# Conditioning of a hybrid decoder layer: eight output tiles per accumulation, one K tile per piece, and six turns instead of 24

## The chip, the cores and the metric

The kernel runs on one core of a Trainium2 chip. A core has five engines that each run their own list of instructions in order and meet only at semaphores: TensorE (PE, with its weight loads shown as PEld), VectorE (DVE), ScalarE (ACT), GpSimd (POOL) and SyncE (SP), which here only issues transfers. Sixteen DMA engines move data between the memory (HBM) and the on-chip memory (SBUF). Matrix products land in PSUM, in banks that hold 512 floats for each of 128 partitions. The metric is the device time in microseconds (us), median of several runs.

## The reference

One inference step of one decoder layer on 1024 prompt rows and 8 sample rows, width 1024, all in float32. Every sequence has a conditioning vector `c` (1 prompt and 8 samples, so 9 of them), from which shift, scale and gate of both halves of the layer come:

```python
mod = jax.nn.silu(c) @ w_ada + b_ada                  # (9, 1024) @ (1024, 6144)
sh1, sc1, gt1, sh2, sc2, gt2 = jnp.split(mod[:, None, :], 6, axis=-1)
h = rmsnorm(x, norm1_g) * (1.0 + sc1) + sh1
proj = h @ w_in                                       # then RG-LRU, mLSTM and pooling groups
...
mix = jnp.concatenate([y_a, y_b, y_c], axis=-1) @ w_out
x = x + gt1 * mix
h2 = rmsnorm(x, norm2_g) * (1.0 + sc2) + sh2
x = x + gt2 * (jnp.square(jax.nn.relu(h2 @ w_ff1)) @ w_ff2)
y = rmsnorm(x, final_g)
```

`w_ada` is 25 MB, read once. The change touches only how `mod` is computed.

## The kernel before, in words

Activations lie feature-major: 8 feature tiles (KT) of 128 partitions by 1032 tokens, in three chunks of 344 tokens. The big products run in float32r as three products (high by high, low by high, high by low) of tiles called H_hi, H_lo, W_hi, W_lo (L2407 to L2409), into banks called D. `WV` are the weights of the value heads (L2434 to L2436).

The conditioning gives 48 output tiles (NADA) of 128 features by 9 vectors. The weight tile of one output tile is 128 partitions (the K rows of one K tile) by 8 K tiles by 128 features, in HBM as 128 rows of 4096 bytes, 512 KB in all. The kernel before works in 24 pairs of output tiles, and each pair in two halves of four K tiles. A **piece** is one such half: 2 tiles by 4 K tiles by 128 features for each partition, 512 KB, which `load_raw` (L556) reads as rows of 2048 bytes into one of four slots of a ring called RAWW. The same ring also carries the weight tiles of the big products (L561).

In `ada` (L2378) TensorE uses its four groups of 32 columns: group j holds the vectors of K tile j as its weights (CTX, 32 columns wide, 9 of use) and streams the 256 features of the pair. The four groups write partitions 0, 32, 64 and 96 of one bank, and the second half adds onto the first. So the bank holds four partial sums, 9 rows each, by 256 features. ScalarE copies this to ADS (L1297). Two small products, the **turn** (`ada_turn`, L2392), multiply ADS with SEL, a 128 by 9 matrix made once from the identity (L1710), which both turns the result to features by vectors and adds the four partial sums. VectorE adds the bias and writes MOD (`modulation`, L1717); for the scales it then makes (1 + scale) times the norm's weight (L1719).

The order of all work in the first third is written out by hand in the text MIX_ORDER and read by every engine: `ADA:i:h` is a piece (on ScalarE the copy to ADS after the last piece of a group), `ADT` the turn, `ADM` the modulation, `SQ` and `NS` the sum of squares and the norm of a chunk (L1763, L2398, L1257, L1742), `N:c:k` the normalised tile k of chunk c (L1728, L1251, L1252, L1087), `DK:u:c:a:b` K tiles a to b of the dense product of unit u and chunk c, `D` all eight, `W` and `WV` the split of weights in high and low parts, `V` the value heads, `R:n` the load of ring entry n by ScalarE's queue. The rest are steps of the mixers. The first 20 pieces are loaded by SP, each as soon as the piece four before it has been used (`raw_used`), with the tokens (X0T, L802), the first weight tiles (WR, L822) and WV_raw (L817) at fixed places between them (SP_AFTER); the other 28 by ScalarE's queue.

The first 16 output tiles (shift 1 and scale 1) are needed before the first normalised tile; the program starts with their 16 pieces, pairs in the order 0, 4, 1, 5, 2, 6, 3, 7. The other 32 tiles are spread over the dense products that follow, up to about 370 us. The banks X0 to X4 serve all small products; the function `bank_uses` hands them out: pairs in X3 or X4, turns in X1 at the start and in X3 later.

Of the kernel before, what the change touches and what calls it, by code (L numbers as in the profile page):

```python
# [17 lines left out]
ALU = mybir.AluOpType  # L18
# [5 lines left out]
P = 128  # L24
D = 1024
# [26 lines left out]
AH = KT // 2  # L52
NPAIR = NADA // 2
ADA_START = (0, 4, 1, 5, 2, 6, 3, 7)
ADA_FIRST = 2 * len(ADA_START)
# [10 lines left out]
N_SP_RAW = 2 * len(ADA_START) + RAW  # L66
# [21 lines left out]
def unit_of(kind, t):  # L88
# [4 lines left out]
ADA:0:0 ADA:0:1 SQ:0:0 ADA:4:0 ADA:4:1 SQ:0:1 SQ:1:0 ADT:0 ADM:0 ADA:1:0 SQ:1:1 ADA:1:1 ADT:4 ADM:4 NS:0  # L93
ADA:5:0 ADA:5:1 N:0:0 ADT:1 ADM:1 N:0:1 ADA:2:0 ADA:2:1 ADT:5 ADM:5 ADA:6:0 ADA:6:1 ADT:2 ADM:2 N:0:2 ADA:3:0 W:0
    ADA:3:1 ADT:6 N:0:3 W:1 ADM:6 ADA:7:0 ADA:7:1 ADT:3 N:0:4 N:0:5 ADM:3 ADT:7 ADM:7 N:0:6 N:0:7 NS:1
DK:0:0:0:6
WV:0 DK:1:0:0:6
DK:0:0:6:8
WV:1 WV:2 DK:1:0:6:8
ADA:8:0  # L100
# [31 lines left out]
D:4:1 LRUM:0
D:4:2 R:34 W:6
D:5:0 ADT:12 ADM:12 ADA:13:0 ADA:13:1 R:33 LRUC:1
D:5:1
D:5:2 ADT:13 R:35 ADM:13 ADA:14:0 LRUG:1 ADA:14:1
D:6:0 R:37 W:7 ADT:14 LRUA:1 R:36 R:38 ADM:14
D:6:1 LRUM:1
D:6:2 R:40 ADA:15:0
D:7:0  # L140
D:7:1 W:8 ADA:15:1 LRUC:2 R:39
D:7:2 ADT:15 LRUG:2 LRUA:2
D:8:0 R:41 ADM:15 ADA:16:0 W:9
# [24 lines left out]
D:16:0 R:65 HM:7 Y:6 U:7 YD:6 CN:7 ADM:23
# [5 lines left out]
def plan_mix():  # L174

    raws = [("ADA", i, h) for i in ADA_START for h in range(2)]
    pairs = [i for i in range(NPAIR) if i not in ADA_START]
    early, pairs = pairs[:2], pairs[2:]
    raws += [("ADA", i, h) for i in early for h in range(2)]
    for u in range(3, N_MIX):  # L180
        raws += [("W", u)] + [("ADA", pairs[u - 3], h) for h in range(2)]
    assert len(pairs) == N_MIX - 3
# [15 lines left out]
def bank_uses(plan):  # L198
# [8 lines left out]
    for s in plan:  # L207
# [5 lines left out]
        elif k == "ADA" and s[2] == 0:  # L213
            add(("ADA", s[1]), "X3" if s[1] in ADA_START[::2] else "X4")
# [75 lines left out]
def build(nc, I, O):  # L290
# [13 lines left out]
    ADA_ORDER = [k[1] for k in raw_seq if k[0] == "ADA" and k[2] == 0]  # L304
# [10 lines left out]
    with ExitStack() as ctx:  # L315
# [88 lines left out]
        ADS, SEL = at("ADS", [P, 2 * P], rSB), new("SEL", [P, DEC + 1])  # L404
# [87 lines left out]
        ada_half = sem("ada_half")  # L492
        win_lower = [sem(f"windows{j}_lower") for j in range(POOL_T)]
        win_upper, win_joined = sem("windows0_upper"), [sem(f"windows{j}_joined") for j in range(POOL_T)]
        ld_idn, sel_ready = sem("ld_idn"), sem("sel_ready")
# [56 lines left out]
        def load_raw(e, n):  # L552
            key = raw_seq[n]
            if key[0] == "ADA":
                w = AH * P
                e.dma_start(RAWW[:, n % RAW, :].rearrange("p (e n) -> p e n", e=2),  # L556
                            I["WADA"][2 * key[1]:2 * key[1] + 2, :, key[2] * w:(key[2] + 1) * w].rearrange("e p n -> p e n")
                            ).then_inc(raw_in[n % RAW], 16)
            else:
                u = key[1]  # L560
                e.dma_start(RAWW[:, n % RAW, :], I["W"][in_unit(u)]).then_inc(raw_in[n % RAW], 16)  # L561

        def raw_used(e, n):
# [649 lines left out]
        def _(act):  # L1213
# [55 lines left out]
            for s in plan:  # L1269
# [22 lines left out]
                elif k == "ADA" and s[2]:  # L1292
                    i, key = ADA_ORDER.index(s[1]), ("ADA", s[1])
                    if i:
                        wait_full(act, ("ADT", ADA_ORDER[i - 1]))
# [381 lines left out]
        def _(dve):  # L1677
# [32 lines left out]
            V.tensor_reduce(SEL[:], IDN[:].rearrange("p (j i) -> p i j", j=P // 32)[:, 0:DEC + 1, :], AX_X, ALU.add).then_inc(sel_ready, 1)  # L1710

            def modulation(key):

                j, (bk, n) = 2 * key[1], use[key]
                wait_full(dve, key)
                ps = XB[bk][:, 0:32].rearrange("p (e b) -> p e b", e=2)[:, :, 0:DEC + 1]
                put_free(V.tensor_tensor(MOD[:, j:j + 2, :], ps, wide(col("b_ada", j, 2), DEC + 1), ALU.add), key)  # L1717
                if j // KT in (1, 4):
                    link(V.scalar_tensor_tensor(out=MOD[:, j:j + 2, :], in0=MOD[:, j:j + 2, :], scalar=1.0,  # L1719
                                                in1=wide(col("g1" if j < 2 * KT else "g2", j % KT, 2), DEC + 1), op0=ALU.add, op1=ALU.mult))  # L1720
# [638 lines left out]
        def _(pe):  # L2359
# [12 lines left out]
            def ada(i, half):  # L2372

                raw = raw_wait(pe, ("ADA", i, half))
                ps = take(("ADA", i)) if half == 0 else bank(("ADA", i))
                for j in range(AH):
                    k = (AH * half + j) * (DEC + 1)
                    one = T.matmul(ps[32 * j:32 * j + 32, 0:2 * P], CTX[:, k:k + 32],  # L2378
                                   RAWW[:, raw, :].rearrange("p (e k n) -> p e k n", e=2, k=AH)[:, :, j, :],
                                   start=(half == 0), stop=(half == 1), tile_position=(0, 32 * j))  # L2380
                if half:
# [504 lines left out]
```

## Time and profile before

| | |
|---|---|
| median of 3 runs | 1174.8 us (1170.45, 1174.8, 1176.62) |
| profiled execution | 1175.78 us, span 1174.0 us |
| PE busy | 1124.6 us (96%) |
| DVE, ACT, POOL busy | 792.8, 473.4, 346.9 us |
| mean granted clock of TensorE | 0.982 of full |
| HBM read, written | 96.81 MB, 12.18 MB |

The span runs from the first to the last instruction. TensorE is busy 96% of it, so what it does not do in the first 50 us (where transfers are the limit), and what it does beside the big products after that, is what the conditioning can cost. A busy time counts overlapped instructions once; a `matmul` instruction in float32 appears as two records, so one turn (two products) is four records and one piece (four products) eight.

### The profile page before, as it was taken

The numbers are of one execution on the slowest core, as the hardware profiler recorded it, in microseconds if no ns is written. First come the engines' busy times: TensorE is split into PE (matmuls) and PEld (weight loads), VectorE is DVE, ScalarE is ACT, GpSimd is POOL, SyncE is SP. The second block draws the span as 40 slices with busy tenths as digits, with TensorE's granted clock in tenths as the row PEclk, the third lists the DMA queues.
The fourth block names the chain that finished last, engine by engine and source line by source line (L and its number), as shares of the span: only waits on it lengthen the run. The fifth ranks groups of instructions, "written<-read, shape, count | busy, mean of one in ns | idle before, by whom it ended". The sixth has DMA issues, their size and how long they took to land.

```text
span 1174.0 us, 19681 instructions
## 1 busy us (share of the span) xinstructions
PE 1124.6 (96%) x7237; PEld 1077.3 (92%) x7237; DVE 792.8 (68%) x1319; ACT 473.4 (40%) x780; POOL 346.9 (30%) x275
## 2 busy tenths in 40 slices
PE   4799999999989999999999999999999999999997
PEld 1598888888979999899999999999999999999996
DVE  4561455478775434678578878778778788788546
ACT  5551355655456344642233332332432433433431
POOL 0442011201434357764032022132131231231352
PEclk9699999998989999999999999999999999999998
DMA  8912523566523722111111111202102202111104
GB/s 302 326 57 88 142 90 126 177 180 218 176 87 113 269 90 73 54 55 37 37 36 55 54 37 55 71 18 71 56 16 75 68 18 72 53 50 58 37 1 145
DMA packets 67846, 109.85 MB, mean 94 GB/s; under 512 B 6435, under 2 KB 42567, under 8 KB 67399
## 3 DMA queue, kind: packets, MB, share of 16 engines
q1 hardware_dynamic: 57574, 84.88, 22.0%
q10 hardware_dynamic: 10208, 24.12, 6.6%
q8 instruction: 41, 0.67, 0.2%
q14 instruction: 23, 0.18, 0.0%
HBM read 96.81 MB, written 12.18 MB: 93 GB/s over the span
## 4 chain that ended last, share of the span: by engine, by line
PE 82%; DVE 9%; ACT 3%; DMA 2%; issue 1%; POOL 1%; SPq 1%; ACTq 0%; POOLq 0%; DVEq 0%
PE D L2407 7%; PE D L2409 7%; PE D L2408 7%; PE D L2591 6%; PE D L2593 5%; PE D L2592 5%; PE X L2593 5%; PE X L2591 5%; PE X L2592 5%; PE X L2663 5%; PE X L2664 5%; PE X L2665 5%; PE D L2663 2%; PE D L2665 2%; PE D L2664 2%; DMA RAWW<-in_WADA 2%
## 5 line engine op out<-in xcount | busy, mean ns | idle before, releaser
L2407 PE MATMUL D<-H_hi,W_hi 128*128 128x344 f32 x472 | 158.6, 336 | 3.7 <-POOL H_lo L1087 3.1
L2409 PE MATMUL D<-H_hi,W_lo 128*128 128x344 f32 x472 | 152.4, 323 | 0.0
L2408 PE MATMUL D<-H_lo,W_hi 128*128 128x344 f32 x472 | 152.4, 323 | 0.0
L1087 POOL TENSOR_TENSOR Y_lo<-FU,Y_hi 128x344 fp32r<-128x344 f32 (+3 forms) x84 | 100.1, 1194 | 154.2 <-ACT Y_hi L1521 88.5
L1082 POOL TENSOR_TENSOR W_lo<-RAWW,W_hi 128x1024 fp32r<-128x1024 f32 x25 | 61.6, 2465 | 182.5 <-ACT W_hi L1234 182.2
L1087 POOL TENSOR_TENSOR Y_lo<-EY,Y_hi 128x344 fp32r<-128x344 f32 (+1 forms) x24 | 38.3, 1598 | 216.3 <-ACT Y_hi L1521 144.5
L2407 PEld LDWEIGHTS D<-H_hi,W_hi 128*128 128x128 f32 x472 | 90.5, 192 | 11.8 <-issue 7.6
L2408 PEld LDWEIGHTS D<-H_lo,W_hi 128*128 128x128 f32 x472 | 90.3, 191 | 0.9 <-issue 0.5
L2409 PEld LDWEIGHTS D<-H_hi,W_lo 128*128 128x128 f32 x472 | 90.2, 191 | 0.0
L2215 DVE SCALAR_TENSOR_TENSOR X<-X,MOD 128x344 f32<-128x344 f32 (+1 forms) x138 | 75.7, 566 | 9.2 <-PE X L2665 9.0
L2663 PE MATMUL X<-Y_hi,W_hi 128*128 128x344 f32 x252 | 80.7, 320 | 0.0
L2664 PE MATMUL X<-Y_lo,W_hi 128*128 128x344 f32 x252 | 80.6, 320 | 0.0
L2665 PE MATMUL X<-Y_hi,W_lo 128*128 128x344 f32 x252 | 80.5, 319 | 0.0
L2017 DVE SCALAR_TENSOR_TENSOR X<-D,MOD,X 128x344 f32<-128x344 f32 (+1 forms) x72 | 41.3, 573 | 45.4 <-PE D L2593 24.7
L2407 PE MATMUL D<-Y_hi,W_hi 128*128 128x344 f32 x192 | 62.0, 323 | 1.5 <-POOL W_lo L1082 1.5
L1099 POOL TENSOR_TENSOR SS<-SS,SQ 128x344 f32<-128x344 f32 x45 | 43.3, 963 | 65.9 <-ACT SQ L1430 40.5
L1087 POOL TENSOR_TENSOR Y_lo<-KEPT,Y_hi 128x344 fp32r<-128x344 f32 x24 | 26.4, 1098 | 120.7 <-ACT Y_hi L1521 120.7
L2408 PE MATMUL D<-Y_lo,W_hi 128*128 128x344 f32 x192 | 61.3, 319 | 0.0
L2409 PE MATMUL D<-Y_hi,W_lo 128*128 128x344 f32 x192 | 61.3, 319 | 0.0
L1556 ACT ACTIVATE W_hi<-RAWW 128x1024 fp32r<-128x1024 f32 x30 | 31.8, 1059 | 64.3 <-PE X L2665 55.6
L2378 PE MATMUL X<-RAWW,CTX 128*32 128x256 f32 x384 | 35.7, 461 | 19.5 <-DMA RAWW<-in_WADA 19.4
L1087 POOL TENSOR_TENSOR H_lo<-FU,H_hi 128x344 fp32r<-128x344 f32 (+2 forms) x33 | 29.9, 914 | 66.2 <-ACT FU L1252 50.7
(416 smaller groups left out, 3455.1 us busy)
## 6 DMA issues: line engine op xcount, KB each, us to landing
RAWW<-in_W SPq DMA_DIRECT2D x76, 512.0 KB, 3.6
RAWW<-in_WADA ACTq DMA_DIRECT2D x28, 512.0 KB, 4.1
RAWW<-in_WADA SPq DMA_DIRECT2D x20, 512.0 KB, 8.0
RAWW<-in_W ACTq DMA_DIRECT2D x18, 512.0 KB, 3.7
X0T<-in_x SPq DMA_DIRECT2D x3, 1376.0 KB, 12.8
out_y<-OUTN SPq DMA_DIRECT2D x24, 172.0 KB
X<-in_x SPq DMA_DIRECT2D x8, 344.0 KB, 5.3
NM<-nm_d SPq DMA_DIRECT2D x8, 256.0 KB, 5.3
```

Source lines behind the costliest of these rows:

```text
L1082: nc.gpsimd.tensor_tensor(lo_v, RAWW[:, raw, :] if src is None else src[:], hi_v.bitcast(F32), ALU.subtract).then_inc(w_lo_ready, 1)
L1087: nc.gpsimd.tensor_tensor(lo_v, fu_v, hi_v.bitcast(F32), ALU.subtract).then_inc(lo_ready, 1)
L2215: V.scalar_tensor_tensor(out=X[:, m, c * CH:c * CH + w], in0=ps[:, 0:w], scalar=MOD[:, 5 * KT + m, 0:1], in1=X[:, m, c * CH:c * CH + w], o ...
L2407: T.matmul(out, w_h, hi[:, kt, a:b], start=(kt == 0), stop=False)
L2408: T.matmul(out, w_h, lo[:, kt, a:b], start=False, stop=False)
L2409: one = T.matmul(out, w_l, hi[:, kt, a:b], start=False, stop=(kt == KT - 1))
L2591: T.matmul(out, w_h, hi(kt), start=(kt == 0 and not onto), stop=False, skip_group_check=onto)
L2592: T.matmul(out, w_h, lo(kt), start=False, stop=False, skip_group_check=onto)
L2593: one = T.matmul(out, w_l, hi(kt), start=False, stop=(kt == n - 1), skip_group_check=onto)
L2663: T.matmul(bank[:, 0:CH], w_hi[:, a:a + P], h, start=(start and k == 0), stop=False, skip_group_check=onto)
L2664: T.matmul(bank[:, 0:CH], w_hi[:, a:a + P], l, start=False, stop=False, skip_group_check=onto)
L2665: one = T.matmul(bank[:, 0:CH], w_lo[:, a:a + P], h, start=False, stop=(stop and k == 1), skip_group_check=onto)
```

## The change

A group now is eight output tiles, and a piece is one K tile of all eight: group j of TensorE's columns streams tiles 2j and 2j+1, 256 features, all with the same weights, the vectors of this K tile. Eight pieces add up in the bank (K is summed wholly in PSUM), so the four column groups hold four finished pairs of output tiles and no partial sums. There are 6 groups of 8 pieces (48 pieces, as before), 6 copies to ADS, 6 turns and 6 modulations. The turn now picks columns 0 to 8, 32 to 40, 64 to 72 and 96 to 104 of the identity, 36 columns, and SEL is gone. The modulation writes 72 columns at once. The first two groups hold the even and the odd ones of the first 16 output tiles.

A piece has the same 512 KB, but its rows in HBM are now 512 bytes (one K tile of 128 features of one output tile), 1024 of them instead of 256 of 2048 bytes. The output tiles of one piece lie 512 KB apart, in the first two groups 1 MB.

```diff
-AH = KT // 2
-NPAIR = NADA // 2
-ADA_START = (0, 4, 1, 5, 2, 6, 3, 7)
+K_PIECE = 1
+GROUPS = 4 // K_PIECE
+ADA_T = 2 * GROUPS
+N_PIECE = KT // K_PIECE
+N_ADA = NADA // ADA_T
+N_START = 2 * KT // ADA_T
...
-ADA:0:0 ADA:0:1 SQ:0:0 ADA:4:0 ADA:4:1 SQ:0:1 SQ:1:0 ADT:0 ADM:0 ADA:1:0 SQ:1:1 ADA:1:1 ADT:4 ADM:4 NS:0
...
+ADA:0:0 ADA:0:1 SQ:0:0 ADA:0:2 ADA:0:3 SQ:0:1 SQ:1:0 ADA:0:4 ADA:0:5 SQ:1:1 NS:0 ADA:0:6 ADA:0:7 ADT:0 ADM:0
...
-DK:0:0:0:6
-WV:0 DK:1:0:0:6
-DK:0:0:6:8
-WV:1 WV:2 DK:1:0:6:8
+DK:0:0:0:1 DK:0:0:2:3 DK:0:0:4:5 DK:0:0:6:7 DK:0:0:1:2 DK:0:0:3:4
+WV:0 DK:1:0:0:1 DK:1:0:2:3 DK:1:0:4:5 DK:1:0:6:7 DK:1:0:1:2 DK:1:0:3:4
+DK:0:0:5:6 DK:0:0:7:8
+WV:1 WV:2 DK:1:0:5:6 DK:1:0:7:8
...
         elif k == "ADT":
-            add(s, "X1" if s[1] in ADA_START else "X4" if s[1] == NPAIR - 1 else "X3")
+            add(s, "X1" if s[1] < N_START else "X4" if s[1] == N_ADA - 1 else "X3")
...
-                add(("TS", w), ("X3", "X4")[w])
+                add(("TS", w), ("X3", "X2")[w])
...
+    def ada_tiles(q):
+
+        return slice(q, 2 * KT, N_START) if q < N_START else slice(ADA_T * q, ADA_T * (q + 1))
...
-                w = AH * P
-                e.dma_start(RAWW[:, n % RAW, :].rearrange("p (e n) -> p e n", e=2),
-                            I["WADA"][2 * key[1]:2 * key[1] + 2, :, key[2] * w:(key[2] + 1) * w].rearrange("e p n -> p e n")
+                w = K_PIECE * P
+                e.dma_start(RAWW[:, n % RAW, :].rearrange("p (t n) -> p t n", t=ADA_T),
+                            I["WADA"][ada_tiles(key[1]), :, key[2] * w:(key[2] + 1) * w].rearrange("t p n -> p t n")
...
-            V.tensor_reduce(SEL[:], IDN[:].rearrange("p (j i) -> p i j", j=P // 32)[:, 0:DEC + 1, :], AX_X, ALU.add).then_inc(sel_ready, 1)
...
+            def ada(q, piece):
+
+                raw = raw_wait(pe, ("ADA", q, piece))
+                ps = take(("ADA", q)) if piece == 0 else bank(("ADA", q))
+                w = RAWW[:, raw, :].rearrange("p (t h n) -> p t h n", t=ADA_T, h=K_PIECE)
+                for j in range(4):
+                    g, h = j // K_PIECE, j % K_PIECE
+                    k = (piece * K_PIECE + h) * (DEC + 1)
+                    one = T.matmul(ps[32 * j:32 * j + 32, 0:2 * P], CTX[:, k:k + 32], w[:, 2 * g:2 * g + 2, h, :],
+                                   start=(piece == 0), stop=(piece == N_PIECE - 1), tile_position=(0, 32 * j))
...
+                pick = IDN[:].rearrange("p (g b) -> p g b", g=GROUPS)[:, :, 0:DEC + 1]
                 for e in range(2):
-                    one = T.matmul(ps[:, 16 * e:16 * e + DEC + 1], ADS[:, e * P:(e + 1) * P], SEL[:], start=True, stop=True)
+                    out = ps[:, 64 * e:64 * e + GROUPS * (DEC + 1)].rearrange("p (g b) -> p g b", g=GROUPS)
+                    one = T.matmul(out, ADS[:, e * P:(e + 1) * P], pick, start=True, stop=True)
```

**The start, on TensorE.** The program of before, from its first piece (X<-RAWW,CTX, eight rows for two pieces) to the first dense product (D<-H_hi,W_hi):

```order
L2378 MATMUL X<-RAWW,CTX 32x256 x16
L2392 MATMUL X<-SEL,ADS 128x9 x2
L2378 MATMUL X<-RAWW,CTX 32x256 x8
L2392 MATMUL X<-SEL,ADS 128x9 x2
L2398 MATMUL X<-SS,ONE 128x344
L2378 MATMUL X<-RAWW,CTX 32x256 x8
...
L2378 MATMUL X<-RAWW,CTX 32x256 x8
L2392 MATMUL X<-SEL,ADS 128x9 x4
L2398 MATMUL X<-SS,ONE 128x344
L2407 MATMUL D<-H_hi,W_hi 128x344
```

And the same stretch now, where the two rows of the identity (X<-IDN,ADS) are the turns of the first and the second group:

```order
L2386 MATMUL X<-RAWW,CTX 32x256 x24
L2407 MATMUL X<-SS,ONE 128x344
L2386 MATMUL X<-RAWW,CTX 32x256 x8
L2401 MATMUL X<-IDN,ADS 128x36 x2
L2386 MATMUL X<-RAWW,CTX 32x256 x32
L2401 MATMUL X<-IDN,ADS 128x36 x2
L2407 MATMUL X<-SS,ONE 128x344
L2416 MATMUL D<-H_hi,W_hi 128x344
```

Eight turns have become two, the sum of squares of the first chunk stands after six pieces, and the second turn and the sum of squares of the second chunk stand between the last piece and the first dense product.

**The start, on VectorE.** Before, from the sums of squares (SS) to the end of the first chunk's normalised tiles (FU), each modulation (MOD) between them:

```order
L1763 TENSOR_TENSOR SS<-SS,SQ 128x344 x12
L1717 TENSOR_TENSOR MOD<-X,COLS 128x18
L1763 TENSOR_TENSOR SS<-SS,SQ 128x344 x4
L1717 TENSOR_TENSOR MOD<-X,COLS 128x18
L1719 SCALAR_TENSOR_TENSOR MOD<-MOD,COLS 128x18
L1742 RECIPROCAL X<-SS 128x344
L1728 SCALAR_TENSOR_TENSOR FU<-X0T,MOD,X 128x344
...
L1728 SCALAR_TENSOR_TENSOR FU<-X0T,MOD,X 128x344
L1732 TENSOR_SCALAR FU<-FU,MOD 128x344
L1742 RECIPROCAL X<-SS 128x344
```

And now:

```order
L1769 TENSOR_TENSOR SS<-SS,SQ 128x344 x16
L1748 RECIPROCAL X<-SS 128x344
L1720 TENSOR_TENSOR MOD<-X,COLS 128x8x9
L1726 SCALAR_TENSOR_TENSOR MOD<-MOD,COLS 128x4x9
L1734 SCALAR_TENSOR_TENSOR FU<-X0T,MOD,X 128x344 x4
L1738 TENSOR_SCALAR FU<-FU,MOD 128x344
L1720 TENSOR_TENSOR MOD<-X,COLS 128x8x9
L1726 SCALAR_TENSOR_TENSOR MOD<-MOD,COLS 128x4x9
L1734 SCALAR_TENSOR_TENSOR FU<-X0T,MOD,X 128x344 x4
L1738 TENSOR_SCALAR FU<-FU,MOD 128x344
L1748 RECIPROCAL X<-SS 128x344
```

The four even tiles of the first chunk follow the first modulation, the four odd ones the second.

**Later, on TensorE.** One of the 12 turns that go after the start, before: it stands between a product of the mLSTM and its next one (VB_105 is a buffer of values, KW the weighted keys).

```order
L2392 MATMUL X<-SEL,ADS 128x9 x2
L2528 MATMUL X<-VB_105,KW 96x97 x4
L2378 MATMUL X<-RAWW,CTX 32x256 x4
L2498 MATMUL X<-IDN,K_1_102 128x96 x4
L2502 MATMUL X<-Q_1_104,K_1_102 128x128 x4
```

And now:

```order
L2537 MATMUL X<-VB_105,KW 96x97 x4
L2386 MATMUL X<-RAWW,CTX 32x256 x4
L2507 MATMUL X<-IDN,K_1_102 128x96 x4
L2511 MATMUL X<-Q_1_104,K_1_102 128x128 x4
```

The turn is gone, and each piece stands where one stood before.

## Rows read from the trace of the kernel before

**Rows 1.** Busy time by stretch: us, each engine's, clock, DMA share, GB/s.
```profile
4.00:22.00 18.00, 7.45 (x52) 2.16 (x52) 7.98 (x23) 9.40 (x20) 0.00 (x0) 1.00 1.05 379
...
24.00:26.00 2.00, 2.00 (x17) 0.60 (x16) 0.75 (x4) 1.83 (x2) 0.00 (x0) 1.00 0.73 238
26.00:28.00 2.00, 1.92 (x25) 0.94 (x20) 2.00 (x1) 0.38 (x1) 0.00 (x0) 1.00 0.42 143
28.00:30.00 2.00, 0.75 (x8) 0.69 (x12) 1.73 (x6) 1.11 (x3) 0.00 (x0) 0.90 0.63 235
30.00:36.00 6.00, 1.23 (x12) 0.23 (x12) 0.10 (x1) 1.16 (x3) 1.83 (x2) 0.50 0.94 320
...
60.00:235.00 175.00, 170.72 (x1111) 152.14 (x1109) 81.94 (x146) 79.67 (x137) 36.72 (x25) 1.00 0.36 114
235.00:345.00 110.00, 100.14 (x731) 93.42 (x730) 86.25 (x175) 53.30 (x75) 25.95 (x19) 0.96 0.52 163
```

**Rows 2.** Chain of waits, 0 to 62 us: start, us, what.
```profile
28.80 10.01 DMA RAWW<-in_WADA
...
41.13 2.00 DVE MOD L1719
...
45.45 1.35 PE X L2398 x2
46.79 0.29 PE D L2407
```

**Rows 3.** Timeline around the last piece of the start: start, us, engine, line, what.
```profile
36.69 1.02 PE L2392 MATMUL X<-SEL,ADS 128*128 128x9 f32 x4
...
40.81 1.94 PE L2378 MATMUL X<-RAWW,CTX 128*32 128x256 f32 x16
...
41.44 0.43 PEld L2378 LDWEIGHTS X<-RAWW,CTX 128*32 128x32 f32 x8 [0.42 <-DMA RAWW<-in_WADA]
```

**Rows 4.** Busy time by stretch, while only rows of 512 bytes were read.
```profile
258.00:258.25 0.25, 0.25 (x4) 0.25 (x3) 0.21 (x2) 0.00 (x0) 0.00 (x0) 1.00 1.05 317
258.25:258.50 0.25, 0.25 (x3) 0.25 (x2) 0.22 (x2) 0.00 (x0) 0.00 (x0) 1.00 1.06 312
258.50:258.75 0.25, 0.25 (x4) 0.25 (x3) 0.22 (x2) 0.00 (x0) 0.00 (x0) 1.00 1.14 346
```

**Rows 5.** DMA view of 257.0 to 259.5 us, two such loads from first to last.
```profile
DMA packets 899, 0.55 MB, mean 219 GB/s; under 512 B 32, under 2 KB 899, under 8 KB 899
```

**Rows 6.** Line L1297, all records: duration ns min/median/max, first and last start.
```profile
L1297 ACT ACTIVATE ADS<-X x24: 358/384/385, 12.8 to 365.4; 128x256 f32<-128x256 f32 x24
```

**Rows 7.** Timeline of TensorE around one turn at 140 us.
```profile
140.04 0.32 PE L2409 MATMUL D<-H_hi,W_lo 128*128 128x344 f32 x1
140.19 0.51 PE L2392 MATMUL X<-SEL,ADS 128*128 128x9 f32 x4
140.55 0.40 PE L2407 MATMUL D<-H_hi,W_hi 128*128 128x344 f32 x1
140.79 0.32 PE L2408 MATMUL D<-H_lo,W_hi 128*128 128x344 f32 x1
```

**Rows 8.** Waits of TensorE, 100 to 385 us: us in total, times, longest.
```profile
PE X L2549 <- DVE NUM L1903: 3.7, 1, 3.7
...
PE X L2536 <- DVE MOD L1717: 1.5, 1, 1.5
...
PE X L2392 <- DVEq L1941: 0.9, 1, 0.9
...
PE X L2392 <- DVE QK L1875: 0.4, 1, 0.4
PE X L2458 <- DVE MOD L1717: 0.3, 1, 0.3
```

**Rows 9.** Lines L962 and L966, all transfers of each, from issue to landing.
```profile
DMA to landing us min/median/max: 3.3/3.5/4.7
DMA to landing us min/median/max: 3.4/3.6/4.4
```

More of the change, by code:

```diff
@@ L132 @@
+D:1:2 ADA:2:4 G1 ADA:2:5
+D:2:0 R:24
+D:2:1 R:26 G2
+D:2:2 R:28 W:4 G3 ADA:2:6 R:27 R:29
+D:3:0 ADA:2:7 G4
+D:3:1 R:31 ADT:2 LRUC:0
+D:3:2 ADM:2 W:5 ADA:3:0
+D:4:0 R:30 ADA:3:1 LRUG:0 R:32 LRUA:0
 D:4:1 LRUM:0
 D:4:2 R:34 W:6
-D:5:0 ADT:12 ADM:12 ADA:13:0 ADA:13:1 R:33 LRUC:1
+D:5:0 ADA:3:2 ADA:3:3 R:33 LRUC:1
 D:5:1
-D:5:2 ADT:13 R:35 ADM:13 ADA:14:0 LRUG:1 ADA:14:1
-D:6:0 R:37 W:7 ADT:14 LRUA:1 R:36 R:38 ADM:14
+D:5:2 R:35 ADA:3:4 LRUG:1 ADA:3:5
+D:6:0 R:37 W:7 LRUA:1 R:36 R:38
 D:6:1 LRUM:1
-D:6:2 R:40 ADA:15:0
+D:6:2 R:40 ADA:3:6
@@ L174, in plan_mix @@
 def plan_mix():
[L176 to L179, printed above, removed]
+    pieces = [("ADA", q, k) for q in range(N_ADA) for k in range(N_PIECE)]
+    raws, pieces = pieces[:N_SP_RAW], pieces[N_SP_RAW:]
     for u in range(3, N_MIX):
-        raws += [("W", u)] + [("ADA", pairs[u - 3], h) for h in range(2)]
-    assert len(pairs) == N_MIX - 3
+        raws += [("W", u)] + pieces[2 * (u - 3):2 * (u - 2)]
+    assert len(pieces) == 2 * (N_MIX - 3)
     out = []
@@ L213, in bank_uses @@
         elif k == "ADA" and s[2] == 0:
-            add(("ADA", s[1]), "X3" if s[1] in ADA_START[::2] else "X4")
+            add(("ADA", s[1]), "X3" if s[1] < N_START and s[1] % 2 == 0 else "X4")
         elif k == "ADT":
-            add(s, "X1" if s[1] in ADA_START else "X4" if s[1] == NPAIR - 1 else "X3")
+            add(s, "X1" if s[1] < N_START else "X4" if s[1] == N_ADA - 1 else "X3")
         elif k in ("G1", "G2", "G3", "G4", "Y", "YS"):
@@ L403, in build @@
         CTS = at("CTS", [P, CW], rH)
-        ADS, SEL = at("ADS", [P, 2 * P], rSB), new("SEL", [P, DEC + 1])
+        ADS = at("ADS", [P, 2 * P], rSB)
         COLS, IDN, ONE = new("COLS", [P, NCOLS]), new("IDN", [P, P]), new("ONE", [P, P])
@@ L1291, in _ @@
                     load_raw(act, s[1])
[L1292 to L1295, printed above, removed]
+                elif k == "ADA" and s[2] == N_PIECE - 1:
+                    key = ("ADA", s[1])
+                    if s[1]:
+                        wait_full(act, ("ADT", s[1] - 1))
                     wait_full(act, key)
@@ L2370, in done @@
                 ins.then_inc(x_full[use[key][0]], 1)
[L2372 to L2381, printed above, removed]
-                    done(one, ("ADA", i))
+            def ada(q, piece):
[7 more added lines that the diff above has]
+                                   start=(piece == 0), stop=(piece == N_PIECE - 1), tile_position=(0, 32 * j))
+                if piece == N_PIECE - 1:
+                    done(one, ("ADA", q))
                 else:
-                    one.then_inc(ada_half, 1)
+                    one.then_inc(ada_piece, 1)
             def ada_turn(key):
```

100 lines of the change are left out of this document (47 added, 53 removed).

## The prediction

> **What bounds the kernel now.** I read the busy time by stretch first, then the chain of waits, then TensorE's waits and its timeline around the turns. There are three regimes. In the first 46 us TensorE waits for transfers: from 4 to 22 us the 16 DMA engines are full, 379 GB/s at a share of 1.05 [rows 1], and a wait of 10.01 us for a piece lies on the chain [rows 2]. From 60 to 235 us TensorE itself is the bound, busy 170.72 of 175.00 us; from 235 to 345 us it is busy 100.14 of 110.00 us [rows 1] and shares the bound with VectorE, for which it waits up to 3.7 us at a time [rows 8]. After 385 us nothing of the conditioning is left and nothing moves. So the change has two sides: the start, where only bytes, rows of transfers and the tail behind the last piece count, and the middle, where each instruction taken off TensorE counts.
>
> **The middle, what goes.** 24 copies to ADS [rows 6] go with 24 turns. Eight are at the start, 16 later; now 2 and 4. So 12 turns leave the middle. What one costs is read where nothing waits: from the start of the product before it, 140.04, to the second product behind it, 140.79, is 0.75 us [rows 7]. Two products without a turn would take two steps of 0.15 to 0.16 (the first row and the turn start 0.15 apart), 0.32 us. A turn costs 0.43 us, and 12 cost 5.2 us. With them go waits that only a turn has, or that its bank makes for others: 0.9 and 0.4 us before a turn, 1.5 us where a transpose of HM waits for the modulation to free X3, 0.3 us where the gate transposes do [rows 8]; 3.1 us together. Upper bound: 8.3 us.
>
> Not all of it reaches the end. Two of the 12 turns (at about 241 and 321 us in the timeline) stand where TensorE comes too early for VectorE anyway, and the wait of 3.7 us for NUM [rows 8] shows that a TensorE ahead of time finds VectorE late. I take off two turns, 0.9 us, and keep 7.4 us. Lower bound: 7 of the 12 turns lie before 235 us, where TensorE is the bound, 3.0 us. The four turns that stay stream 36 columns instead of 9; I cost this at nothing, since the weights (128 columns, twice per product) are loaded as before and cover it, and at most 0.1 us each if they don't. VectorE loses 18 modulations and ScalarE 18 copies of 0.384 us [rows 6]; beside TensorE, they only help the waits counted.
>
> **The middle, what comes.** 32 pieces, less the four that SP loads, now are 1024 rows of 512 bytes each. Before, from 258.00 to 258.75 us only rows of 512 bytes were moved, back to back: 317, 312 and 346 GB/s, mean 325, at a share of 1.05 to 1.14 [rows 4]. A piece has 524,288 bytes: 1.38 us at 379 GB/s, 1.61 us at 325, so 0.23 us more. 32 of them hold the engines 7.4 us longer. The share is 0.36 before 235 us and 0.52 in the mLSTM stretch [rows 1], where keys, queries and the values of a chunk come by the same engines. TensorE waited for no piece there. If every added microsecond met a waiting load, it would be 7.4 times 0.52, 3.8 us; if none, 0. I take +1.0, nearer to none, for no piece was late.
>
> **The start.** The first dense product needs all 16 pieces, as before, for the turn of the second group stands ahead of it. The pieces are 8.39 MB beside 3.9 MB of tokens and weights. 16 times 0.23 is 3.7 us more of transfer. Against it stands a hole: from 24 to 30 us the engines moved 238, 143 and 235 GB/s instead of 379 [rows 1], a shortfall of 141, 236 and 144 GB/s over 2 us each, or 2.7 us of full transfer. It came from the ring: SP loads a piece when the one four before it is used, and TensorE sat behind turns, a modulation and the sum of squares. In the new order six pieces stand before the sum, and no turn stands between pieces 1 and 8, so I expect the hole to be filled. Last piece: +1.0 us, between 2.1 - 2.7 = -0.6 (at 346 GB/s) and +3.7 (nothing filled).
>
> Then the tail. The last piece was there at 41.4 us [rows 3], and dense products flow alone from 46.79 [rows 2]: 5.4 us, with two turns, a modulation that took 2.00 us [rows 2] and the sum of squares in between. Now: the piece 1.0 us (two took 1.94 [rows 3]), the copy 0.38 [rows 6], one turn 1.02 [rows 3], the sum 1.35 [rows 2], some 0.3 for the semaphores between: 4.1 us, so -1.3. These are prices at the low clock level: the granted clock is 0.50 from 30 us [rows 1], that is 1.2 GHz, after TensorE had little to do, and I expect the same again. What the odd tiles add: four instead of two normalised tiles are still open when the dense products begin. The first dense products use the even tiles, 12 products at 0.29 us [rows 2], 3.5 us; an odd tile comes after the modulation (2.0 us if it meets GpSimd again) and the steps of one tile on three engines. That is a near thing, and the norm of the second chunk and WV_lo come behind it. Bounds 0 and +2; I take +0.8, the lower half, since the even tiles stand first. The start: +1.0 - 1.3 + 0.8 = +0.5 us.
>
> A rule of the Trainium skill bears on this term, DMA: Bandwidth & Descriptors, "Why small descriptors are slow (HBM only)": a packet costs about three cycles beside one for each 32 bytes. By it 2048 bytes take 67 cycles and four times 512 take 76, 13% more; the rows of this trace say 17% (379 against 325). As an estimate from that page, the last piece would come 1 us earlier than by the rows.
>
> **Sum.** -7.4 + 1.0 + 0.5 = -5.9 us against the profiled execution, 1175.8 us: 1169.9. The median of the runs shown lies 1.0 us lower, 1174.8; so 1168.9, say 1169.
>
> **Rivals.**
> *A slower start, and a slower kernel.* The rows of 512 bytes of one partition lie 512 KB or 1 MB apart, and the rate may fall under what the back-to-back stretch showed. The price: over the whole of two such loads the mean was 219 GB/s, with their beginning and end in it [rows 5]. At that rate a piece takes 2.39 us, 1.01 more; 16 of them 16.2 us, less the hole 2.7 and the tail 1.3, plus 0.8: start +13.0, in all -7.4 + 1.0 + 13.0 = +6.6, 1181.4 on the scale of the median. The kernel gets slower from the point where a piece takes 0.60 us more, at 265 GB/s. Against it: line L966 loads rows 1 MB apart of 1024 bytes, and they land in 3.6 us, 0.1 more than whole rows of 4096 [rows 9].
> The Trainium skill speaks for it, same page, "Latency and other measured facts", on a row pitch of large powers of two: 207 GB/s at a pitch of 512 KiB, 164 at 2 MiB, against 214. As an estimate from this page, a piece of the start would take up to 1.3 times as long as its rows say, some 2.1 us; rows 9 don't show it at a pitch of 1 MB.
> *The turns come off TensorE, and VectorE gives nothing.* Only the 7 turns before 235 us count: -3.0 + 0.5 + 1.0 = -1.5, 1173.3. For it: the wait on NUM in that stretch, VectorE busy 86.25 of 110.00 us. Against it: VectorE is fed by TensorE, and loses work as well.
> *Everything comes through.* -8.3, the start at its good end -0.6 - 1.3 = -1.9, no late loads: -10.2, 1164.6. For it: 96% busy TensorE overall. Against it: it needs three good ends at once.
> That the change doesn't do what it says, fewer turns, I exclude: TensorE's program has the 6.
>
> **How the numbers follow.** Forecast 0.43, own range 1166 to 1172. Slower start 0.13. VectorE gives nothing 0.28. Everything 0.16. A measurement of this kernel can tell about 0.5%, 5.9 us, from no change: below 1168.9 is faster, above 1180.7 slower. The forecast lies on that line; I give 0.25 of its 0.43 to faster and 0.18 to same, since its unpriced remainders (turns at the low clock) go down. Faster: 0.25 + 0.16 = 0.41. Slower: 0.11 of the slower start's 0.13. Same: 0.18 + 0.28 + 0.02 = 0.48. The range 1163.5 to 1179.5 reaches past "everything" and towards the slower start, without its end.
>
> **What would show it.** The rate from 4 to 22 us: 325 to 340 GB/s, and no hole from 24 to 30. The last piece of the start at 42 to 43 us, TensorE's first dense product alone at 47 to 48. Six copies to ADS. At 235 us the same work 2.5 to 3.5 us earlier than before; at 385 us about 6 us earlier. A piece in the first 50 us at 2 us or more makes the slower start right; a lead at 235 us of 3 us that is gone by 385 makes VectorE the one that took it. Waits of TensorE for pieces after 60 us, or longer ones for keys and values, would say that +1.0 was too little.

## The result, and the profile after

The changed kernel takes 1180.77 us (median of 13 runs, 1175.48 to 1183.6), the kernel before 1174.39 beside it: ratio 1.0044, interval [1.0029, 1.006]. It is 5 to 6 us slower where 6 us faster was forecast, and lies outside the range. The interval lies wholly above 1: a small loss, but a clear one. The profiled execution took 1181.2 us, its span is 1179.3; before they were 1175.8 and 1174.0.

The step was made as described. ScalarE copies ADS six times:
```profile
L1300 ACT ACTIVATE ADS<-X x6: 374/383/386, 28.2 to 370.9; 128x256 f32<-128x256 f32 x6
```

The busy time by stretch (columns as in [rows 1]) shows the new rate of the transfers, and where the clock fell:
```profile
4.00:22.00 18.00, 4.77 (x39) 1.04 (x40) 7.36 (x21) 8.31 (x16) 0.00 (x0) 1.00 1.12 324
...
24.00:26.00 2.00, 2.00 (x14) 0.66 (x10) 0.90 (x2) 1.64 (x3) 0.00 (x0) 1.00 1.20 289
26.00:28.00 2.00, 1.93 (x16) 0.25 (x12) 1.40 (x1) 0.50 (x1) 0.00 (x0) 1.00 1.20 290
...
60.00:235.00 175.00, 167.66 (x1071) 149.34 (x1069) 80.52 (x138) 79.99 (x134) 38.98 (x26) 1.00 0.37 112
235.00:345.00 110.00, 104.48 (x726) 97.46 (x727) 83.88 (x161) 49.34 (x66) 24.67 (x18) 0.91 0.58 169
345.00:385.00 40.00, 36.13 (x228) 31.90 (x227) 27.39 (x55) 23.99 (x39) 17.57 (x16) 0.91 0.38 107
```
The hole from 24 to 28 us is gone (before 238 and 143 GB/s, [rows 1]), but it is filled at 290 GB/s, with the engines at a share of 1.20. A piece of 524,288 bytes takes 1.81 us at that rate, not the 1.61 of [rows 4]; before, in a stretch with nothing but pieces of 2048-byte rows, the rate was 388 GB/s:
```profile
20.00:22.00 2.00, 1.61 (x16) 0.20 (x8) 1.82 (x5) 1.58 (x5) 0.00 (x0) 1.00 1.06 388
```

The chain of waits at the end of the start (start us, us, what):
```profile
28.99 8.45 DMA RAWW<-in_WADA
...
38.62 6.19 DMA RAWW<-in_WADA
...
44.85 1.13 PE X L2386 x8
...
46.06 0.39 ACT ADS L1300
...
46.50 1.07 PE X L2401 x4
47.57 1.30 PE X L2407 x2
48.87 0.29 PE D L2416
```
The last piece lands at 44.81 us instead of 41.4. Behind it stand 4.06 us to the dense products (forecast 4.1), which flow from 48.87 us instead of 46.79. (The profile of before is a late one here: two other profiles of the old order with 2048-byte rows have this product 1.2 and 1.5 us earlier, so the start may have lost up to 3.6 us.)

How far the same product of TensorE lies from its place before, read from the two timelines (us, minus is earlier):
```
place before    57    100   126-150  155-205   209-218  226   241   262   288   312   325   385 to the end
after          +2.3  +1.7   +0.5    -0.7..+0.1  +0.9   -0.3  +4.8  +3.4  +3.1  +1.6  +5.6   +5.6
```
So up to 205 us the fewer turns paid back the 2.3 us that the start had lost. Then 5.9 us were lost between 226 and 325 us. Nothing moves behind 385 us, as forecast.

TensorE's waits, 100 to 385 us (us in total, times, longest), against [rows 8]:
```profile
PE X L2529 <- DVE EX L1901: 3.9, 2, 2.2
PE X L2558 <- DVE NUM L1909: 3.7, 1, 3.7
PE X L2507 <- DMA VB<-v_d: 2.9, 1, 2.9
...
PE X L2551 <- DVE KW L1898: 1.3, 1, 1.3
```
For each chunk of the mLSTM, EX are the weighted scores, KW the weighted keys and NUM the numerators of its output, all three made by VectorE, and VB are its values, loaded from HBM. Two rows of before belong beside these:
```profile
PE X L2520 <- DVE EX L1895: 2.9, 3, 1.7
PE X L2498 <- DMA VB<-v_d: 0.9, 1, 0.9
```
The waits that belonged to turns and modulations are gone. What is left is VB, 2.9 us, at 235 us (0.9 before, at 244); EX, 2.2 us, at 272 (1.7 before, at 268); KW, 1.3 us, at 318, which is new; EX, 1.7 us, at 341; and NUM, 3.7 us, at 350, as before. From 200 to 360 us all waits together are 12.9 us, where they were 10.9. At four of them, VB, EX at 272, KW and NUM, the granted clock is at its lower level, 0.50 (1.2 GHz), the first three here:
```profile
232.00:237.00 5.00, 2.09 (x27) 1.44 (x20) 0.75 (x3) 1.59 (x2) 0.00 (x0) 0.99 0.77 188
237.00:243.00 6.00, 5.99 (x30) 5.18 (x23) 4.01 (x10) 0.63 (x1) 0.00 (x0) 0.50 1.08 328
...
271.00:277.00 6.00, 5.29 (x24) 5.30 (x25) 4.03 (x10) 2.26 (x3) 1.65 (x1) 0.50 0.55 186
277.00:318.00 41.00, 39.91 (x304) 36.50 (x302) 36.93 (x69) 18.38 (x27) 9.55 (x7) 0.99 0.78 228
318.00:325.00 7.00, 6.83 (x31) 6.84 (x32) 4.89 (x11) 2.29 (x2) 4.66 (x4) 0.56 0.08 24
```
Each of these low stretches lasts some 7 us, and there products take twice the time: 3.5 us more where TensorE has work all the while. The profile of before has two of the four, at EX (268.5 to 275.5 us) and at NUM (343.5 to 350.5). Those at VB and KW are new. Summed as (1 - granted clock) over stretches of 1 us from 200 to 360 us, the profile after has lost at most 13.7 us, that of before 6.8. So the two new low stretches, 6.9 us, weigh more than the 2.0 us of longer waits. One execution is a sample only: the kernel's own runs lie 8 us apart.

### The profile page after: what moved, and what is told of

Read it like the earlier page. It is cut to its first block, busy times and chain, and to the rows that moved or that the text cites. A ratio compares the mean times of both kernels' runs of the same rounds, so it can differ in the third digit from the quotient of the medians.

```text
span 1179.3 us, 19438 instructions
## 1 busy us (share of the span) xinstructions
PE 1122.1 (95%) x7165; PEld 1072.1 (91%) x7165; DVE 789.4 (67%) x1295; ACT 467.5 (40%) x762; POOL 347.8 (29%) x275
## 4 chain that ended last, share of the span: by engine, by line
PE 79%; DVE 9%; DMA 4%; ACT 4%; POOL 1%; issue 1%; SPq 1%; ACTq 0%; POOLq 0%; DVEq 0%
PE D L2416 6%; PE D L2418 6%; PE D L2417 6%; PE D L2600 6%; PE D L2602 5%; PE D L2601 5%; PE X L2602 5%; PE X L2600 5%; PE X L2601 5%; PE X L2672 5%; PE X L2673 5%; PE X L2674 5%; DMA RAWW<-in_WADA 3%; PE D L2672 2%; PE D L2674 2%; PE D L2673 2%
## 5 line engine op out<-in xcount | busy, mean ns | idle before, releaser
L1102 POOL TENSOR_TENSOR SS<-SS,SQ 128x344 f32<-128x344 f32 x45 | 43.3, 963 | 65.9 <-ACT SQ L1433 40.5
L2386 PEld LDWEIGHTS X<-RAWW,CTX 128*32 128x32 f32 x384 | 8.5, 119 | 45.5 <-DMA RAWW<-in_WADA 28.7
```

## Experiments

**The size of the rows, in either order.** Only the layout of the weights on the host and the source of the transfer change:
```diff
-                            I["WADA"][ada_tiles(key[1]), :, key[2] * w:(key[2] + 1) * w].rearrange("t p n -> p t n")
+                            I["WADA"][N_PIECE * key[1] + key[2]].rearrange("h p n -> p h n")
```
with h = 2 (2048 bytes), h = 1 (4096), or h = 8 (512 bytes, but 64 KB apart). In the kernel before, the same is done the other way: the four K tiles and two output tiles of a piece are read as eight rows of 512 bytes, 512 KB apart, or as one of 4096.

> The changed kernel, whose pieces lie on the host so that a row has 2048 bytes (two per partition) as before the change; bytes, order, products and turns are those of the changed kernel. Theory rows (the 512-byte rows cost the time): a piece takes 1.38 instead of 1.81 us, the last piece of the start lands at 38 to 40 us instead of 44.8, the dense products flow alone at 43 to 45, the values' piece waits less at 235 us, and the time is 1165 to 1169, 12 to 16 us less than the changed kernel. Rival order (where the pieces and turns stand in the middle costs it, not their rows): only the start moves, 4 to 5 us, 1176. Rival turns (they never gave anything): not under 1174.

> The changed kernel with rows of 512 bytes still, but the eight rows of a partition lie 64 KB apart and those of neighbouring partitions one behind the other, where in the changed kernel they lie 1 MB (start) or 512 KB (later) and 4 KB apart. Theory number of rows: a piece of the start takes 1.8 us as in the changed kernel, 290 GB/s from 22 to 30 us, and the time is 1179 to 1182. Rival pitch: the rate is that of the 512-byte stretch of the kernel before, 325 GB/s or more, a piece 1.61 us, the last piece of the start 3 us earlier, the time 1175 to 1178.

> The kernel before, with all its 24 turns and its own order, but its pieces come in rows of 512 bytes (eight per partition, 512 KB apart) as in the changed kernel. Theory rows: a piece takes 1.8 us instead of 1.38, 16 of them 6.9 us more, of which the hole from 24 to 30 us takes some 2.7: start +4 to +5, and the middle +1 to +6; the time is 1179 to 1185. Rival order: only the start's part, 1177 to 1179, and no wait of 2 us or more for a transfer of the values near 235 us.

> The kernel before with its pieces laid out so that each partition reads one row of 4096 bytes (before: two of 2048). Theory rows: if 512 to 2048 bytes gives 290 to 379 GB/s, the next doubling gives at most 3 per cent, a piece 0 to 0.05 us less, the time 1172 to 1175. Rival: rows of 2048 still cost at the start, the last piece lands 1 us or more earlier, 1172 or less.

Measured, as ratio to the kernel before:
```
rows of      order before             order after
512 bytes    1.0036 [1.0023, 1.0050]  1.0044 [1.0029, 1.0060]   (64 KB apart: 1.0057 [1.0035, 1.0080])
2048         1                        0.9970 [0.9953, 0.9988]
4096         0.9983 [0.9968, 0.9998]  0.9968 [0.9949, 0.9986]
```
With 2048-byte rows the change makes the kernel faster, 1170.56 us, 10 us less than with 512 (9 by the ratios). The expectation's 1165 to 1169 was too good by 2. Read along a line of the table, with the same rows in both orders, the new order is worth -1 us with 512-byte rows (within the intervals), 3.5 us with 2048 and 2 us with 4096 (its intervals overlap). So with short rows nearly the whole loss against the kernel before is theirs: the old order loses 4 us by them as well. Stretches of before_rows512, after_rows512_near and after_rows2048, one row each:
```profile
22.00:24.00 2.00, 1.28 (x12) 0.20 (x8) 1.79 (x6) 1.70 (x4) 0.00 (x0) 1.00 1.20 291
```
```profile
22.00:24.00 2.00, 1.27 (x16) 0.20 (x8) 1.69 (x5) 1.59 (x5) 0.00 (x0) 1.00 1.20 290
```
```profile
4.00:22.00 18.00, 6.81 (x49) 1.64 (x50) 8.91 (x25) 9.74 (x20) 0.00 (x0) 1.00 1.04 380
```
290 GB/s belongs to the row of 512 bytes in both orders, and it is the same whether the rows of a partition lie 1 MB or 64 KB apart. The rival of the pitch falls. The figures that the prediction cites from the Trainium skill (DMA: Bandwidth & Descriptors, "Latency and other measured facts") are for a large pitch from one partition's row to the next; here those rows lie 4 KB and 512 bytes apart, so no run here tests them, and they didn't bear on this rival. The rule of the Trainium skill on small packets (DMA: Bandwidth & Descriptors, "Why small descriptors are slow (HBM only)") had the direction. The prediction's reading of it, 13% more, was less than half of what was measured: pieces land 1.80 us apart with 512-byte rows and 1.36 with 2048, 33% more. (The 380 GB/s above has the tokens in it; over the same 18 us the changed kernel moved 324.)

**Where the long rows count.**
```diff
+                if n < N_SP_RAW:        # after_long_later: n >= N_SP_RAW
+                    e.dma_start(RAWW[:, n % RAW, :], I["WADAP"][N_PIECE * key[1] + key[2], 0]
+                                ).then_inc(raw_in[n % RAW], 16)
+                else:
```

> The changed kernel, where the 20 pieces that SP loads (16 of the start, 4 of the next group) come as one row of 4096 bytes per partition and the 28 later ones as 512-byte rows as in the changed kernel. Theory both ends (the start pays 6 of the 10 us between short and long rows, the mLSTM stretch the rest): start 4.1 us before that of the kernel before, 6.5 at 205 us, then 2 to 4 us given up from 235 to 345 us; 1172 to 1176. Rival start alone: all of the 10 us lie in the start, the time is that of long rows everywhere, 1170 to 1171.

> The other half: the 20 pieces that SP loads come in 512-byte rows as in the changed kernel, the 28 later ones as one row of 4096 bytes per partition. Theory both ends: start 2.2 us late as in the changed kernel, level with the kernel before at 205 us, and nothing or 2 us lost from 235 to 345 us; 1175 to 1178. Rival start alone: as the changed kernel, 1180 to 1181.

> The changed kernel with all pieces as one row of 4096 bytes per partition. Theory: 390 instead of 380 GB/s at the start, dense products alone at 41.5 to 43 us, otherwise as with rows of 2048; 1168 to 1171. Rival: rows of 2048 have all there is, 1170.5 again. Beside after_long_start and after_long_later it says whether their two gains add up.

Measured: long rows at the start 1171.52 (0.9984 [0.9972, 0.9997]), only later 1178.57 (1.0030 [1.0012, 1.0047]), everywhere 1171.79 (0.9968 [0.9949, 0.9986]). By the ratios the start is worth 7 us, the later pieces 1.6 to 1.9 (the medians give 9.3 and 2.2, and 0 with a long start). The profiles agree. In the six of the changed order with 4096-byte rows at the start (and no products added there) the first dense product starts at 40.5 to 43.5 us, 41.9 in the mean (by the timeline, which has it 0.7 us ahead of the chain above); in the five with 512-byte rows at 48.0 to 48.5. That is 6.3 us. The start decides, as the rival had it, and the later rows cost 0 to 2 us: the +1.0 of the forecast was about right.

**The wait for the values.** SP loads VB of chunk 0 before it waits for the last queries:
```diff
                     if c == 0:
+                        for i in range(2):
+                            sp.wait_ge(v_stored[i], 16 * NLC // 2)
+                        sp.dma_start(VB[0][:].rearrange("p h v -> p (h v)"), v_d[0]).then_inc(ld_kqv[0], 16)
```

> The changed kernel with 512-byte rows; SP loads the values of the first chunk (VB) before it waits for the last queries to be stored, some 5 us earlier, and K, Q and NM as before. Theory wait: TensorE's wait of 2.9 us for VB at 235 us goes, K and Q then bound it; 1.5 to 2.5 us of the loss in the mLSTM stretch come back, 1178 to 1179.5. Rival: K or Q land no earlier and the wait goes over to them, or VectorE takes it, 1180 to 1181.

> The changed kernel with rows of 4096 bytes and the values of the first chunk loaded before the wait for the last queries. Theory wait: TensorE's waits for VB at 223 to 238 us go, and with them a drop of the clock; 1 to 2.5 us less than with rows of 4096 alone, 1169 to 1171. Rival: K and Q bound it at the same place, 1171 to 1172.

Measured: 1178.22 with 512-byte rows (1.0041 [1.0028, 1.0055]), 1170.87 with 4096 (0.9962 [0.9944, 0.9981]), both within the intervals of the kernels without the edit. The medians lie 2.6 and 0.9 us lower, in the theory's ranges, but each stands against its own runs of the kernel before, and the ratios differ by 0.0003 and 0.0006 only: the times don't tell. The wait for VB is gone from both profiles. In its place TensorE waits 1.1 us for EX at the next step, and in the second one 2.2 us for EX at 258 us. By the traces the rival is right: take one wait away, and the next one on VectorE's side ends last.

**Products in place of waits.** If the loss is the low clock behind the waits, TensorE must not stand still there. 50 products with zeros are added, which change no value:
```diff
+            FILL = {("S", 0): 6, ("S", 1): 6, ("AB", 0): 6, ("AB", 2): 4, ("YS",): 10, ("AB", 6): 8, ("POOL", 0, 0): 10}
+            def fill(s):
+                for _ in range(FILL.get(s, 0)):
+                    T.matmul(XB["X4"][:, 0:P], IDN[:], ZERO[:, 0:1].to_broadcast([P, P]), start=False, stop=False)
...
+                    fill(s)
                     pe.wait_ge(x_free[bk], n + 1)
```

> The changed kernel (512-byte rows) with 50 products of the identity with zeros (128 columns each, some 0.16 us) that TensorE makes where it waited in the changed order's mLSTM stretch: 6 ahead of K of chunks 0 and 1, 6 and 4 ahead of EX of chunks 0 and 2, 10 ahead of the HS transposes, 8 ahead of EX of chunk 6, 10 ahead of the first pool product. They add zeros to the open sum in X4. Theory clock (TensorE comes early, waits for VectorE or for VB, and behind each such wait its clock is granted at 0.50 for 3.4 to 7 us, which costs more than the wait): the waits are filled, the granted clock between 230 and 345 us stays 1.00 but for one drop at most, and 3 to 5 us come back, 1176 to 1178. Rival: the products come on top, 8 us of them where 10 us of waits were; the time is 1180 to 1184.

> The same 50 products in the changed kernel with rows of 4096 bytes. Theory clock: 2 to 4 us come back, 1168 to 1170, and the scatter between executions (1163.7 to 1174.2 without) gets smaller, for it would come from how long the clock stays low. Rival: they come on top, 1173 to 1176.

> Rows of 4096 bytes, values early, and the 50 products together. Theory clock: the best of these, 1166 to 1169. Rival: no better than rows of 4096 alone, 1171 to 1173.

Measured: with rows of 4096 bytes 1166.31 (1164.53 to 1167.77; 0.9928 [0.9904, 0.9951]), with the values early as well 1165.38 (0.9916 [0.9891, 0.9941]). The products take 5.5 us off the kernel with rows of 4096 bytes (4.7 by the ratios), and the spread of its runs shrinks from 10.6 us (12 runs) to 3.2 (6 runs). The same place in the timelines, after_rows4096 first:
```profile
301.73 0.64 PE L2386 MATMUL X<-RAWW,CTX 128*32 128x256 f32 x8
304.39 0.32 PE L2551 MATMUL X<-IDN,HS 8*128 8x8 f32 x3 [2.02 <-DVE KW L1898]
```
```profile
301.77 2.50 PE L2410 MATMUL X<-ZERO,IDN 128*128 128x128 f32 x20
304.20 0.35 PE L2562 MATMUL X<-IDN,HS 8*128 8x8 f32 x3
```
One product takes some 0.24 us, not the 0.16 expected, and the ten just fill the wait. The product behind doesn't come earlier by this; what differs is the clock of the stretch that follows (last three columns: clock, share, GB/s), again without and with the products:
```profile
302.00:310.00 8.00, 5.97 (x40) 5.62 (x33) 7.16 (x14) 2.30 (x2) 6.16 (x7) 0.80 0.28 94
...
334.00:341.00 7.00, 5.91 (x14) 4.00 (x15) 6.30 (x12) 5.79 (x11) 4.29 (x4) 0.51 0.53 159
```
```profile
302.00:310.00 8.00, 8.00 (x63) 7.86 (x63) 6.87 (x12) 2.30 (x2) 6.16 (x7) 1.00 0.21 76
...
334.00:341.00 7.00, 5.68 (x36) 4.96 (x35) 6.21 (x10) 6.23 (x11) 4.33 (x4) 1.00 0.81 215
```
The clock stays at 1.00 from 200 to 400 us in both filled kernels with long rows. The two executions shown differ by 1 us only, for the one without the products was among the fast ones of its kernel (1165.6, median 1171.8). What speaks for the clock in the other 5 us is its mean in each execution: without the products, the three fastest of twelve (1163.7 to 1167.0 us) had 0.986 to 0.988, the nine others (1170.2 to 1174.2) 0.974 to 0.982; the six with them had 0.985 to 0.989. The mean takes in the start as well, so it doesn't say where the clock was low. With 512-byte rows the products gave little: 1179.18 (1.0030 [1.0011, 1.0050]), under 2 us, less than the 3 to 5 expected. Its profile still has a wait that I had not filled, for a late piece, and the clock falls behind it at 244 us:
```profile
PE X L2387 <- DMA RAWW<-in_WADA: 2.2, 1, 2.2
```
It falls again at 347 us, for 7 us, behind the waits that the ten products ahead of the pool product did not cover (NUM, 1.5 us, and one for ScalarE, 1.4). That is one sample. What else keeps this kernel's runs 8 us apart is open; their mean granted clocks don't follow their times.

**What the turns are worth with the clock held.** The order before needs its products at other places, where X4 holds no open sum; a first try moved turn 22 to make room.
```diff
-D:14:2 POOL:0:0 POOLS:1 NU:6 YD:3 R:60 POOLY:0:0 POOL:0:1 ADT:22 POOLY:0:1
+D:14:2 ADT:22 POOL:0:0 POOLS:1 NU:6 YD:3 R:60 POOLY:0:0 POOL:0:1 POOLY:0:1
+            FILL = {("S", 1): 2, ("AB", 0): 6, ("AB", 2): 10, ("ADT", 20): 5, ("Y", 2): 8, ("POOL", 0, 0): 18}
```

> The kernel before (24 turns, rows of 2048 bytes) with 49 products of the identity with zeros where its TensorE waited in the mLSTM stretch: 6 and 10 ahead of EX of chunks 0 and 2, 2 ahead of K of chunk 1, 5 ahead of turn 20, 8 ahead of the third HM transpose, 18 ahead of the first pool product; turn 22 moved ahead of that product, so that they have a bank. Theory clock plus turns (the low clock behind waits costs both orders; the turns' own 0.43 us each are real): the clock stays 1.00, 2 to 4 us come back, 1170.5 to 1172.5, and the changed order keeps an advantage. Rival order's fault (only the changed order suffered from the clock): no gain, 1174 to 1176.

> The same with rows of 4096 bytes; to be held against the changed order with rows of 4096 and its filled waits, 1166.3. Theory turns real: 1169 to 1171, so with rows and clock taken out the six turns instead of 24 are worth 3 to 5 us. Rival (turns are worth nothing even then): 1166 to 1167.5.

Measured: 1179.69 and 1177.08, slower than without, and neither theory is served. The timeline of before_fill shows why:
```profile
343.24 0.99 PE L2394 MATMUL X<-SEL,ADS 128*128 128x9 f32 x4 [4.89 <-DVEq L1942]
344.08 6.49 PE L2402 MATMUL X<-ZERO,IDN 128*128 128x128 f32 x36
350.41 1.32 PE L2562 MATMUL X<-ST,BDP 128*128 128x344 f32 x4
```
The moved turn waits 4.89 us for bank X3, the clock falls, and the 18 products then run at 1.2 GHz with nothing left to fill, for 6.5 us. Up to 338 us the same products of TensorE came 2.7 us earlier than in the kernel before, of which 1.3 were there from the start; behind this place they come 3.3 us later. Without the move and those 18 (and in the changed order without the 10 at the same place):

> The kernel before (rows of 2048 bytes) with 31 of the 49 products of before_fill, without the 18 ahead of the pool product, and with turn 22 where it was: in before_fill the moved turn waited 4.89 us for X3 and the 18 products came on top behind it, which made that run say nothing on the turns. Theory clock plus turns: up to 336 us before_fill had gained 1.3 us over its start; 1172 to 1173.5. Rival: 1174 to 1176.

> The same with rows of 4096 bytes. Theory turns real: 1170 to 1172, 3 us or more above after_rows4096_fill_s. Rival (the turns are worth nothing once the clock is held): within 1.5 us of it.

> The changed kernel with rows of 4096 bytes and its products but for the 10 ahead of the pool product, so that both orders are filled at the same kind of places (K, EX, X3) and neither ahead of the pool. One fall of the clock, behind the pool's wait, comes back in both. Theory: 1167 to 1169, 1 to 2 us more than with all 50.

Measured: 1172.91 (0.9975 [0.9961, 0.9989]), 1171.61 (0.9967 [0.9950, 0.9983]) and 1167.71 (0.9922 [0.9900, 0.9943]). With the clock held at all places but one (0.50 for 7 us behind NUM in each of the three), the changed order is 3.9 us ahead of the order before, 5.3 by the ratios, whose intervals don't overlap. Its start has some of that: with 4096-byte rows the first dense product comes at 43.1 to 43.5 us in the order before and at 41.9 in the mean in the changed one. The two last profiles, in the form of the table above (changed order against order before):
```
place before_rows4096_fill_s   60     97    121    157    217    229    235    271    307    344
after_rows4096_fill_s         -0.7   -1.5   -2.6   -3.0   -3.3   -4.5   -0.4   -2.0   -3.7   -1.6
```
The lead grows as turns go, by 3.8 us from 60 to 229 us. At 235 us it is nearly nothing: before chunk 0 TensorE waits for VB and EX in the one and not in the other. (The profiles end 1.6 us apart, not 3.9: the one of the changed order was the slowest of its six executions.) The waits of after_rows4096_fill_s there, 222 to 240 us:
```profile
PE X L2539 <- DVE EX L1902: 1.9, 1, 1.9
PE X L2516 <- DMA VB<-v_d: 0.4, 1, 0.4
```
Six products ahead of K, 1.4 us, stand there too, which the order before doesn't have. I read from it that what went ahead of chunk 0 was worth nothing, for TensorE then met the loading of the values and VectorE's EX; no run takes only those turns away.

**The low clock at the start.** 24 more such products between pieces 2 and 7 of the second group.

> The changed kernel with rows of 4096 bytes, values early and the 50 products, and 24 more at the start between pieces 2 and 7 of the second group, where TensorE waits 4.4 us for a piece and its clock falls to 0.50. Theory: the turn (1.07 us), the sum (1.3 us) and the first dense products (0.29 us each) run at the full clock, 1 to 2 us less than the 1165.4 without them. Rival: the products meet pieces that came earlier and add, or the odd tiles bound the start, 1165 to 1167.

Measured: 1164.13 (0.9908 [0.9888, 0.9927]), 1.3 us under the kernel without them. The intervals overlap, so this is not told apart. Its profile has the clock at 1.00 from 30 to 40 us, where it was 0.50, and the first dense product comes 0.7 us earlier. It is the fastest version, 11 us under the kernel before, and 17 under the change as it was made.

## Why the prediction was wrong

- **Which step failed: "what goes" in the middle, 7.4 us.** Up to 226 us the trace gave 2.6 us of it, near the 3.0 forecast for the 7 turns before 235 us. The remaining 4.4 (five turns and the 3.1 us of waits before turns and modulations, less the 0.9 taken off) gave nothing, and between 226 and 325 us 5.9 us were lost in the profile. I took two turns off for "TensorE comes too early for VectorE"; it held for all that lay in the mLSTM stretch. In place of the waits that left, those for VB and EX grew and one for KW came, and I had not asked for each of them what is late next.
- **What I didn't price at all: the clock behind a wait.** [Rows 1] showed 0.96 for 235 to 345 us, and I read no cost from it. The filled kernels show it: 5.5 us with rows of 4096 bytes in the changed order, or 4.1 without the ten products ahead of the pool; 1.2 us in the order before (by the ratios 1.9, and 2.9 with rows of 2048). The changed kernel waits 2.0 us more than before from 200 to 360 us, and two more low stretches cost it up to 6.9 us.
- **The rows, priced at 4.7 us (3.7 at the start, 1.0 later), measured 9 to 10.** That is after_rows2048 against the change as it was made. It is nearly all in the start, and explains 4 to 5 us of the miss of 12; the middle has the rest.
- **The start, +0.5, measured +2.1.** The hole was filled and the tail was 4.06 us, both as forecast. The last piece came at +3.4 instead of +1.0, because a piece took 1.81 us: three stretches of 0.25 us [rows 4] were no measure for a queue that is full for 25 us. The bound of +3.7 held it. The odd tiles, +0.8, cost +0.2. Against the changed order with 2048-byte rows, whose first dense product starts at 42.2 us, the short rows cost 5.9 us there, not 3.7; with 2048-byte rows the start's other terms, +0.5 - 3.7 = -3.2, come out at -3.8.
- **Later transfers, +1.0**: 0 to 2 us by the two halves. Right.
- **The rivals.** "A slower start, and a slower kernel" gave the nearest time, 1181.4, but for a start of +13.0, and a piece took 0.43 us more, short of the 0.60 from which it was to decide. That its time came out was luck: its start was too long by 11 us, and its middle was a gain of 6.4 us that never came. Its price, 2.39 us for a piece, came from [rows 5], which I read as two whole loads; they are parts of three (K, Q and VB, issued from 256.48 us on and landed by 260.25). "VectorE gives nothing" had the place, and stopped at zero where it went below: its -1.5 left the gain before 235 us standing, and the trace shows that this gain was lost as well, at the first load of the values. A rival was missing: that a TensorE ahead of time pays for its earliness, in clock.

## What to carry to other kernels

Before work is taken off the busiest engine, list in order what each following wait would be without it. Work that stands beside a transfer or beside VectorE can be free, and where TensorE then stood still here, the products behind mostly ran at 1.2 GHz. A layout that the host can choose should give each partition long rows: here 2048 bytes in place of 512 turned a change that costs 5 us into one that gives 3.6, and one row of 4096 gave no more. A rate should be read from a stretch in which the queue is full for as long as it will be: 0.75 us showed 325 GB/s, the 8 us from 22 to 30 showed 290. Where TensorE must wait 1 to 3 us in the middle of dense work, products with zeros that end when the wait ends are worth trying, but only where the wait is certain: 18 of them behind the wait and not in it took 6.5 us.

## What the runs showed of the hardware

- Pieces in rows of 512 bytes from HBM moved at 290 GB/s with the DMA engines at a share of 1.20 (after, 24 to 28 us), in rows of 2048 at 388 at 1.06 (before, 20 to 22 us). From 4 to 22 us, with the tokens among the pieces, it was 324 with rows of 512, 380 with 2048 and 391 to 396 with 4096. For rows of 512 bytes, 1 MB or 64 KB between the rows of a partition made no difference (290 both).
- From 200 to 360 us every stretch at a granted clock of 0.50, in every profile, began within 3 us of a wait of TensorE of 1.1 to 4.9 us, and it lasted 3.5 or 7 us, once 10. Not every such wait had one: KW, 2.0 us, had none in after_rows2048, nor had 1.5 us for MOD in the kernel before. With the waits filled by products the clock stayed at 1.00 from 200 to 400 us (rows of 4096 bytes), and the spread between executions fell from 10.6 to 3.2 us.
